# One 512 x 256 block product of each FFN-up pair made from seven inner products, with the token operands by GpSimd

## What is computed

```python
proj = x @ w_in                                   # pool u | q | k | v | o | gates
y_pool = pool_mixer(u_pool); y_ml = sigmoid(o_pre) * mlstm(q, k, v, gates)
x1 = layer_norm(ALPHA * x + concat([y_pool, y_ml]) @ w_out, ln1_g, ln1_b)
ff = square(relu(x1 @ w_ff1 + b_ff1)) @ w_ff2 + b_ff2
x2 = layer_norm(ALPHA * x1 + ff, ln2_g, ln2_b)
```

## Time and profile before

| | |
|---|---|
| median of three runs | 1053.27 us |
| the profiled execution | 1053.31 us |
| its span in the profile | 1051.5 us |
| instructions | 18890 |
| granted clock of TensorE, mean | 0.998 |
| HBM read, written | 104.19 MB, 49.06 MB |

### The profile page before, as it was taken

The page is one execution under the profiler, slowest core; times in us unless marked ns, Lnnn a source line. Parts: engine busy times, 40 slices in busy tenths (PEclk is TensorE's granted clock), DMA queues, the critical chain, the costliest instruction groups (busy, mean ns, idle before and its releaser), DMA issues. The chain is left out here.

```text
span 1051.5 us, 18890 instructions
## 1 busy us (share of the span) xinstructions
PE 1041.0 (99%) x7797; PEld 1028.1 (98%) x7797; DVE 719.3 (68%) x956; ACT 486.6 (46%) x685; POOL 87.5 (8%) x120
## 2 busy tenths in 40 slices
PE   9999999999999999999999999999999999999997
PEld 9999999999899999999999999999999999999985
DVE  6795775536786595855655655658766677887977
ACT  6554434445532576645454554556443323334223
POOL 3112221020211000000000000000000000000027
PEclk9999999999999999999999999999999999999999
DMA  8546996164225211254345345387524415335304
GB/s 284 144 173 156 246 199 130 61 176 114 91 80 159 83 41 55 78 171 152 120 155 165 110 151 168 122 284 254 206 82 151 172 62 182 121 92 171 122 5 157
DMA packets 95154, 148.34 MB, mean 141 GB/s; under 512 B 6164, under 2 KB 51956, under 8 KB 94568
## 3 DMA queue, kind: packets, MB, share of 16 engines
q1 hardware_dynamic: 88290, 127.72, 38.1%
q0 software_dynamic: 6528, 19.19, 7.9%
q10 hardware_dynamic: 270, 0.49, 0.2%
HBM read 104.19 MB, written 49.06 MB: 146 GB/s over the span
## 5 line engine op out<-in xcount | busy, mean ns | idle before, releaser
L2340 PE MATMUL bank<-x_hi,w_hi 128*128 128x344 f32 (+1 forms) x696 | 227.5, 327 | 0.2 <-DVE x_lo L1616 0.2
L2340 PE MATMUL bank<-x_hi,d_lo 128*128 128x258 f32 x968 | 222.4, 282 | 0.0
L2340 PE MATMUL bank<-x_lo,w_hi 128*128 128x344 f32 (+1 forms) x696 | 222.0, 319 | 0.0
L2340 PE MATMUL bank<-x_hi,w_lo 128*128 128x344 f32 x528 | 168.7, 319 | 0.0
L2340 PEld LDWEIGHTS bank<-x_hi,d_lo 128*128 128x128 f32 x968 | 165.7, 189 | 0.0
L2340 PEld LDWEIGHTS bank<-x_hi,w_hi 128*128 128x128 f32 (+1 forms) x696 | 130.4, 187 | 0.9 <-DVE x_lo L1616 0.5
L2340 PEld LDWEIGHTS bank<-x_lo,w_hi 128*128 128x128 f32 (+1 forms) x696 | 130.2, 187 | 0.4
L2340 PE MATMUL bank<-x_lo,s_hi 128*128 128x258 f32 x448 | 126.5, 282 | 0.0
L2340 PE MATMUL bank<-x_hi,s_hi 128*128 128x258 f32 x448 | 126.4, 282 | 0.0
L2340 PEld LDWEIGHTS bank<-x_hi,w_lo 128*128 128x128 f32 x528 | 99.2, 188 | 0.0
L2340 PE MATMUL bank<-t_hi,s_hi 128*128 128x258 f32 x336 | 95.2, 283 | 0.0
(11 more groups left out here) (400 smaller groups left out, 2432.3 us busy)
## 6 DMA issues: line engine op xcount, KB each, us to landing
h_ops<-h_unit SPq DMA_DIRECT2D x56, 258.0 KB, 2.5
x_lo_raw<-h_ops SPq DMA_DIRECT2D x14, 1032.0 KB, 5.3
s_raw<-in_w_ff SPq DMA_DIRECT2D x14, 1024.0 KB, 6.8
x_lo_raw<-h_ops SPq DMA_DIRECT2D x14, 774.0 KB, 4.5
d_raw<-in_w_ff SPq DMA_DIRECT2D x9, 1024.0 KB, 7.8
w_raw<-in_w_in SPq DMA_DIRECT2D x16, 512.0 KB, 7.3
h_ops<-t_out SPq DMA_DIRECT2D x28, 258.0 KB, 5.2
d_raw<-in_w_ff SPq DMA_DIRECT2D x8, 768.0 KB, 6.3
```

What stands on the lines that cost most here:

```text
L2340: return nc.tensor.matmul(out, lhsT, rhs, start=start, stop=stop, skip_group_check=True)
```

## The change

In pairs 1 to 6, the X21 products of the pair's two units (each 128 hidden columns, 512 channels, 516 tokens) become one block product of 256 hidden columns, made by an inner seven-product form with blocks of 128 hidden columns x 256 channels x 258 tokens. `inner` is one such product: 2 chunks x 3 = 6 matmuls into one bank. Seven take the place of 48 matmuls. They stand in the pair's first unit, in the banks `IN_A` and `IN_B` (before, the pair of banks `PC`), and the products are put in another order: X11, X12, inner 1 and 2, XT2, inner 3 and 4, X22, inner 5 and 6, XT3, inner 7, XT4 in the first unit; X11, X12, XT2, X22, XT3, XT4 in the second.

New operands come with it. The inner weights (`iw_raw`, 2 loads of 256 KB a pair on POOL's queue) have their sums (`iw_sums`) and low parts (`iw_los`) by DVE, and their high parts by ACT. The inner token sums (`T1S`, `tq_sum`) and their low parts are made once, by GpSimd, in pair 0. Their space is that of `y_acc`, so GpSimd first stores `y_acc` to DRAM in four transfers and, in the first down operations, loads it back in four. Pair 0 keeps the old products. X11 now counts two on `up_done`, so that a unit still counts seven.

On SP, the store of a unit is split in two (`store_squares`, `store_sums`), and the next unit's weight load stands between them. In the first unit of a pair the even half now comes ahead of h22 on ACT and SP. The waits of the down stage's preparation on the last unit's products are renumbered (+5 becomes +6, +3 becomes +4).

The diff, cut to its core (the new `up_start`, `up_first` of ACT and DVE and the helpers `iw_sums`, `hidden_12` are left out; their rows on DVE are in the fences below):

```diff
--- before
+++ after
+        TPH = at("tq_hi", [P, 3, 2, HB], o_r1, F32R)
+        TPR = at("tq_sum", [P, 3, 2, HB], o_r1 + 6208)
+        TPL = at("tq_lo", [P, 3, 2, HB], o_r1 + 6208, F32R)
+        IWR = at("iw_raw", [P, 4, UW], o_r1 + 12416)
+        IWRL = at("iw_raw_lo", [P, 4, UW], o_r1 + 12416, F32R)
+        IWH = at("iw_hi", [P, NOP, UW], o_r1 + 4 * XROW, F32R)
+        IWS = at("iw_sum", [P, 3, UW], o_r1 + 6 * XROW)
+        IWSL = at("iw_sum_lo", [P, 3, UW], o_r1 + 6 * XROW, F32R)
+        UPB = at("up_b", [P, HALF], o_r1 + 7 * XROW)
+        T1S = Y[:, 7, HALF:NT].rearrange("p (i n) -> p i n", i=2)
...
@@ SP
             load_unit(0, 1)
-            store_unit(0, 0)
+            store_squares(0, 0)
             for j in range(1, NSU // 2):
                 sp.wait_ge(up_done, j * 14 - 7)
                 load_unit(j, 0)
+                store_sums(j - 1, 0)
                 store_last(j - 1, 0)
-                store_unit(j - 1, 1)
+                store_squares(j - 1, 1)
                 sp.wait_ge(up_done, j * 14)
                 load_unit(j, 1)
+                store_sums(j - 1, 1)
                 store_last(j - 1, 1)
-                store_unit(j, 0)
+                store_squares(j, 0)
             u0 = 7 * (NSU - 1)
             sp.wait_ge(up_done, u0)
             load_w(0, A11, DR[0][:, :, :])
...
-            store_unit(NSU // 2 - 1, 1)
+            store_squares(NSU // 2 - 1, 1)
+            store_sums(NSU // 2 - 1, 1)
...
@@ POOL
+            def load_iw(j, ahead=0):
+                for r in range(2):
+                    pool.dma_start(IWR[:, 2 * r:2 * r + 2, :].rearrange("p q (k n) -> p (q k) n", k=2),
+                                   w1_v[:, 4:8, bass.ds(j * (2 * UW) + UW * (NCL + 2 * ahead + r), P)]).then_inc(iw_in, 16)
+            pool.wait_ge(xv_ready, KC * NBLK)
+            for i in range(4):
+                pool.dma_start(y_d[:, 2 * i:2 * i + 2, :], Y[:, 2 * i:2 * i + 2, :]).then_inc(y_out, 16)
+            pool.wait_ge(y_out, DMA0 + 64)
+            pool.wait_ge(t_sum, 5)
+            load_iw(1)
+            b11, b12, b21, b22 = (Y[:, 4 + 2 * (x // 2):6 + 2 * (x // 2), HB * (x % 2):HB * (x % 2 + 1)] for x in range(4))
+            G.tensor_tensor(T1S[:, :, :], b12, b11, ALU.subtract).then_inc(iw_sum, 1)
+            pool.wait_ge(iw_sum, IS0 + 1)
+            G.tensor_tensor(TPR[:, 0, :, :], b22, T1S[:, :, :], ALU.subtract).then_inc(iw_sum, 1)
+            G.tensor_tensor(TPR[:, 1, :, :], b22, b12, ALU.subtract).then_inc(iw_sum, 1)
+            pool.wait_ge(iw_sum, IS0 + 2)
+            G.tensor_tensor(TPR[:, 2, :, :], b21, TPR[:, 0, :, :], ALU.subtract).then_inc(iw_sum, 1)
+            pool.wait_ge(iw_hi, IH0 + 1)
+            G.tensor_tensor(TPL[:, :, :, :], TPR[:, :, :, :], TPH[:, :, :, :].bitcast(F32), ALU.subtract).then_inc(iw_lo, 1)
+            pool.wait_ge(iw_hi, IH0 + 2)
+            pool.wait_ge(up_done, NOP + 2)
+            G.tensor_tensor(XL[:, 4:6, HB:HALF], T1S[:, :, :], XH[:, 4:6, HB:HALF].bitcast(F32), ALU.subtract).then_inc(iw_lo, 1)
+            with pool.Fori(1, NSU // 2 - 1) as j:
+                pool.wait_ge(in_done, at_pair(j)(IN0, N_IN, 8))
+                load_iw(j, 1)
+            pool.wait_ge(in_done, at_pair(NSU // 2 - 1)(IN0, N_IN, 8))
+            pool.wait_ge(up_done, NOP * NSU)
+            for n_done, i in ((0, 2), (4, 0), (8, 1), (8, 3)):
+                if n_done:
+                    pool.wait_ge(dn_done, n_done)
+                    pool.wait_ge(y_in, DMA0 + (16 if i == 0 else 32))
+                rows, cols = slice(4 * (i // 2), 4 * (i // 2) + 4), slice(HALF * (i % 2), HALF * (i % 2 + 1))
+                pool.dma_start(Y[:, rows, cols], y_d[:, rows, cols]).then_inc(y_in, 16)
...
@@ ACT
...
+            def up_second(j, last=False):
+                n, m, r = at_unit(j, 1), at_unit(j, 2), 1
+                up_start(j, r, n)
+                if not last:
+                    iw_hi_raw(j, 1)
+                    iw_hi_sums(j, 1)
+                    s_hi_12(m, 0, 1)
+                    s_hi_34(m, 0)
+                else:
+                    w_hi_part(0)
+                    h_hi_part(0)
+                act.wait_ge(bf_ready, n(1, 1))
+                act.wait_ge(up_added, n(3, 2))
+                hidden_22(n, r)
+                act.wait_ge(up_added, n(3, 3))
+                hidden_even(n, r)
+                if last:
+                    w_hi_part(1)
+                hidden_21(n, r)
...
-                    act.wait_ge(up_done, 7 * (NSU - 1) + 3)
+                    act.wait_ge(up_done, 7 * (NSU - 1) + 4)
...
@@ DVE
+            def iw_los(j):
+                q = at_pair(j)
+                dve.wait_ge(iw_sum, q(IS0 + 4, 4, 4))
+                dve.wait_ge(iw_lo, q(IL0 + 2, 2, 0))
+                dve.wait_ge(iw_hi, q(IH0 + 2, 2, 1))
+                V.tensor_tensor(IWRL[:, :, :], IWR[:, :, :], IWH[:, 0:4, :].bitcast(F32), ALU.subtract).then_inc(iw_lo, 1)
+                dve.wait_ge(iw_hi, q(IH0 + 2, 2, 2))
+                V.tensor_tensor(IWSL[:, :, :], IWS[:, :, :], IWH[:, 4:7, :].bitcast(F32), ALU.subtract).then_inc(iw_lo, 1)
...
+            def hidden_22(n, r, n_half):
+                dve.wait_ge(up_copied, n(4, 2))
+                dve.wait_ge(op_out[B22], n(16, 0))
+                dve.wait_ge(in_done, n_half)
+                V.tensor_tensor(HT[:, 1, HALF:HALF + HB], TMP[:, 0, 0:HB], PA[r][:, 0, 0:HB], ALU.add).then_inc(in_added, 1)
+                dve.wait_ge(up_done, n(7, 6))
+                V.tensor_tensor(HT[:, 1, HALF + HB:NT], TMP[:, 0, HB:HALF], PA[r][:, 1, 0:HB], ALU.add).then_inc(up_added, 1)
...
+            def up_second(j, last=False):
+                n, m, q = at_unit(j, 1), at_unit(j, 2), at_pair(j)
+                s_lo_5(n, 1)
+                dve.wait_ge(up_copied, n(4, 1))
+                dve.wait_ge(in_copied, q(CP0, N_CP, 2))
+                dve.wait_ge(in_added, q(AD0, N_AD, 4))
+                dve.wait_ge(op_out[B11], n(16, 0))
+                dve.wait_ge(t_out, n(4, 0))
+                V.tensor_tensor(HT[:, 0, 0:HALF], UPA, UPB[:, :], ALU.add).then_inc(up_added, 1)
+                s_lo_6(n, 1)
+                if not last:
+                    iw_sums(j, 1)
+                    s_sums(m, 0)
+                s_lo_7(n, 1)
+                hidden_22(n, 1, q(IN0, N_IN, 9))
+                hidden_12(n)
+                if not last:
+                    s_lo_12(m, 0, 1)
+                    s_lo_34(m, 0)
+                else:
+                    w_lo_part(0)
+                    h_lo_part(0)
+                    d_sums(0, 2)
+                    d_sums(0, 1)
+                hidden_sums(n)
...
-                        dve.wait_ge(up_done, 7 * (NSU - 1) + 5)
+                        dve.wait_ge(up_done, 7 * (NSU - 1) + 6)
...
@@ PE
+            def product(out, w_hi, w_lo, x_hi_, x_lo_, start, stop, n_done=1, first_half=None, second_half=None):
 
                 for i in range(2):
+                    if i and first_half is not None:
+                        last.then_inc(first_half, 1)
+                    if i and second_half is not None:
+                        pe.wait_ge(*second_half)
                     o, ns = out[:, i, 0:HB], slice(HB * i, HB * (i + 1))
                     for k in range(4):
                         mm(o, w_hi(k), x_hi_[:, k, ns], start and k == 0, False)
                         mm(o, w_hi(k), x_lo_[:, k, ns], False, False)
                         last = mm(o, w_lo(k), x_hi_[:, k, ns], False, stop and k == 3)
-                last.then_inc(up_done, 1)
+                last.then_inc(up_done, n_done)
...
+            def inner(out, w, x, start, stop):
+                for k in range(2):
+                    cs = slice(P * k, P * (k + 1))
+                    mm(out, w[0][:, cs], x[0][:, k, :], start and k == 0, False)
+                    mm(out, w[0][:, cs], x[1][:, k, :], False, False)
+                    last = mm(out, w[1][:, cs], x[0][:, k, :], False, stop and k == 1)
+                last.then_inc(in_done, 1)
+            def up_first(j):
+                n, q = at_unit(j, 0), at_pair(j)
+                hi, sum_lo, raw_lo = unit_parts(0)
+                pe.wait_ge(s_lo, n(5, 1))
+                pe.wait_ge(up_copied, n(4, -4))
+                product(PA[0], hi(0), raw_lo(0), *X11, True, False, n_done=2)
+                pe.wait_ge(s_lo, n(5, 2))
+                pe.wait_ge(up_added, n(3, 0))
+                product(PD, hi(3), sum_lo(1), *X12, True, False)
+                pe.wait_ge(iw_lo, q(IL0 + 2, 2, 1))
+                inner(IN_A, W11, Q11, True, False)
+                inner(IN_B, W12, Q21, True, True)
+                pe.wait_ge(up_copied, n(4, 1))
+                product(PA[0], hi(2), sum_lo(0), *XT2, False, False)
+                pe.wait_ge(iw_lo, q(IL0 + 2, 2, 2))
+                pe.wait_ge(in_added, q(AD0, N_AD, 1))
+                inner(IN_A, WS2, QT2, False, False)
+                pe.wait_ge(in_added, q(AD0, N_AD, 2))
```

(34 more changed lines are left out.)

## The result

The changed kernel takes 1056.75 us (median of 10 runs, 1054.66 to 1058.87), the kernel before 1053.18 us (10 runs, 1052.91 to 1053.96): a ratio of 1.0032, 95% interval 1.0023 to 1.0041. It is slower by 0.34%, inside the range given (1051.3 to 1057.5), but 2.4 us above the forecast and past the bound of "within 0.2%" (1055.4): "within" had a chance of 0.54, "slower" 0.36. The new kernel also scatters over 4.2 us where the old one scatters over 1.1. The profiled execution took 1057.3 us; its span is 1055.7 us.

What follows compares the result with a forecast made beforehand. TensorE, with matmuls following without a stall, was taken as the bound. Matmuls -4.3, waits in pairs +0.5, GpSimd in pair 0 +2.3 and handover +2.5 gave +1.0 on 1053.31: 1054.3 us, range 1051.3 to 1057.5.

Steps and rivals of the forecast that it cites:

- the matmuls: Pairs 1 to 6: six fewer matmuls a pair, 36 at 0.1201 us each, -4.3 us.
- pair 0: Unit (0,0): GpSimd's four token sums delay VectorE 3.8 us against 1.5 of slack, +2.3 us, between 0 and 3.3.
- the pause: Ahead of the down stage: PE idles 2.9 us for low parts; the handover as a whole +2.5 us.
- C: Rival, handover: the clock falls after PE's idle time; 4 us at 1.2 GHz lose 2.0, so 1056.3 us; chance 0.06.
- E: Rival, pairs: inner 1 comes 0.5 us late in each of five pairs, +2.0 on the forecast, 1056.3 us; chance 0.10.
- one of the signs named for being wrong: Pairs taking over 40 us, where the prediction expected some 39.7 us.
- the later one waits for the earlier: Pair 0, VectorE and GpSimd both reading SBUF: each of four GpSimd sums can push VectorE back by 1.20 us.
- The step on the low part of 1548 elements: Pair 0: GpSimd's 3.6 us low part falls while VectorE waits for unit (1,0)'s weights, costing nothing.
- the chain: VectorE and ScalarE work before inner 1: its low part 0.1 us late in pairs 2 to 6, +0.5 us, between nothing and 2.5.
- SP's loads: SP's queue: moving each weight load ahead of three stores and their t-sum waits costs PE nothing.
- Rival B: Pairs: inner weight loads land over 10.9 us after issue; at 12 us five pairs lose 5.5, so 1059.8 us; chance 0.10.
- Reloading Y: First down operations: four 1 MB loads of the LayerNorm output, due over 15 us after issue, cost nothing, at most +1 us.

Runs made afterwards that it cites:

- e10: Changed kernel with GpSimd's four token sums after unit (0,0)'s h22 sum and the T2 store on GpSimd's queue: 1053.40 us.
- e1: Changed kernel with GpSimd's four token sums held until VectorE has issued the h22 sum of unit (0,0): 1053.96 us.
- e8: Changed kernel with the four token sums moved from GpSimd to VectorE at the same place: 1055.57 us.
- e9: Changed kernel with the old SP order in pairs 1 to 5, t-sum stores ahead of the weight load: 1060.71 us.
- e2: Changed kernel with the T2 store (third t-sum) on GpSimd's queue instead of SP's: 1056.46 us.
- e5: Kernel before with only the change's SP order, each weight load ahead of the three t-sum stores: 1054.39 us.
- e6: Kernel before with down operation 0's two low parts put later on VectorE, so PE pauses ahead of the down stage: 1059.46 us.
- e3: Changed kernel with own space for down operation 0's weights, its hidden operand loaded earlier, VectorE and ScalarE reordered: 1056.56 us.
- e4: Changed kernel with the edits of e1, e2 and e3 together: 1050.78 us.
- e7: e4 with the first loop load behind the stores, unit (6,1)'s last t-sum later, and two LayerNorm-output reloads later: 1049.83 us.

## Why the prediction was right, and where it was not

The parts for the matmuls, pair 0 and the pause held, in mechanism and in size. The time still lies in the range because the range was drawn above rivals C and E: two losses that the sum did not have (1.6 us ahead of XT3, 1.4 by the clock) came on top of it. As far as the first goes that is luck, for no rival named it. And one of the signs named for being wrong came, pairs over 40 us: three of the six take 40.05 to 40.21.

**Matmuls.** -4.3 forecast, -4.3 measured; e10 shows it with the pairs free of waits.

**GpSimd in pair 0.** +2.3 forecast, +2.4 measured, shown by e1 and e8. The step "the later one waits for the earlier", from two rows with selects, holds for sums in both directions, but for the first pair of rows, where VectorE started first by 0.17 us and still was the one that lost. The rule of the Trainium skill (SBUF — State Buffer, Who interferes with whom), that a VectorE instruction with two SBUF inputs and a GpSimd instruction that reads SBUF lock each other out, agrees with VectorE's 3.46 and GpSimd's 3.15 us; and the h11 sum (the row at 439.03), which reads one operand from PSUM, keeps its 0.68 us beside GpSimd's last sum. The step on the low part of 1548 elements was wrong: it does not come "while DVE waits for unit (1,0)'s weights" but costs a t-sum 3.2 us. "Nothing" held only because the weight load no longer stands behind that sum; e9, where it does, loses 5.3 us in that pair, 1.4 of it by the clock.

**Waits in the pairs.** +0.5 forecast ahead of inner 1, which did not come: the chain put VectorE's low part 0.1 us late, and it was 0.2 early, inside the 0.4 to which the chain was said to be good. +1.6 measured ahead of XT3. The step that failed is "*SP's loads* ... PE never waited for these weights: nothing". I asked who waits for the load that was moved, and not who waits for the three stores that it was moved past. One of them frees the buffer of ScalarE's copy of XT2. e2 shows the wait, e5 that the order alone uses up the slack but rarely more, e9 that the old order costs the pairs as much in its profile, by later weights. Rival B, late inner loads, did not come: in the loop they take 3.8 to 7.0 us, where it needed over 10.9.

**The handover.** 2.9 us of pause forecast, 3.0 measured, and down operation 1 does not wait at all, where the sum had 0.15 us.

**The clock.** Rival C, with a chance of 0.06, came true on top of the forecast: 0.50 for 3.1 us, 1.4 us lost, where C had 2.0. The step that failed is the argument from the earlier trace rows: a clock of 1.00 in a window with 0.67 us of matmuls at the kernel's end showed nothing about a pause of 3 us between two stretches of full work. The same view of the kernel before shows the fall in the next 4 us, in which no matmul runs:

```profile
1047.00:1051.00 4.00, 0.00 (x0) 0.00 (x0) 0.54 (x1) 0.00 (x0) 0.00 (x0) 0.52 0.62 197
```

Read 4 us further, these rows would have spoken for C. The Trainium skill (TensorE: Matmul & The Clock Gate, The HAM clock gate) says that an idle array falls back to the lower level; the traces agree, with the pause of 3.0 us here and of 4.8 in e6, though not each time (e9).

**Reloading Y.** Nothing forecast, and nothing seen in the changed kernel's profile. But in e2, e3, e4 and e8 PE waits 0.3 to 0.6 us near 750, behind ScalarE, which waits for the load of a hidden operand. It does not depend on how early PE comes: in e2, e3 and e8 it enters the down stage about as late as in the changed kernel. In e7, with the last two reloads moved, that wait is gone, and one of 1.2 us stands behind another load. That it is the reload that delays these loads wasn't tried alone.

Summed up: the two misses (+1.1 in the pairs, +1.3 behind the pause, where the clock's 1.4 stands) and the 0.5 at the start are 2.9 of the 3.2 us by which the profiled span (1055.7) is above the one forecast (1054.3 - 1.8).

## What to carry to other kernels

When a transfer is moved ahead of others on a queue, ask of each one that it passes who waits for its landing; buffers that are freed by a store count. An engine that was idle 92% of the time isn't free: what it takes from SBUF it takes from its neighbour, so put such work where the neighbour waits, and hold it there by a semaphore. And a pause of 3 us on TensorE can cost half as much again in the lower clock behind it (1.4 us here), so an order of the last block that fits the loop isn't yet one that fits the stage behind it.

## What the runs showed of the hardware that I had not expected

GpSimd's sum of 516 elements takes 1.2 us alone (e1), and 3.15 and 3.34 beside VectorE's low parts: the two engines take turns, instruction by instruction, and both lose. A VectorE sum of 0.70 us took 3.92 and 3.93 when GpSimd's low part of 1548 elements (3.53 us) began some 0.15 us ahead of it. The stretch at the lower clock was seen behind pauses of 2.8 to 4.8 us, not behind one of 2.0 (e3), and once not behind one of 3.0 (e9).
